# A bidirectional Hyena and pooling encoder layer on one core: the modulated input held as four quarters of 512 tokens, the first quarter rounded and subtracted at the end of the filter stage

## What is computed

```python
mod = silu(c) @ w_ada + b_ada
shift, scale, gate = split(mod, 3)
u = h * (1.0 + scale) + shift                 # 2048 tokens x 1024 channels
proj = u @ w_in + b_in                        # 3072 columns
k_freq = rfft(filters(positions) * decay)     # independent of u
y_h = hyena(short_conv(streams), k_freq)      # two long convolutions by FFT
y_p = pool(pool_in)
out = gate * (concat(y_h * silu(hy_gate), y_p * silu(pool_gate)) @ w_out + b_out)
h = layer_norm(alpha * h + out)
```

## Time and profile before

| | us |
|---|---|
| Median of 3 runs | 1243.82 |
| Lowest and highest | 1240.3 and 1246.71 |
| Time of the profiled execution | 1241.09 |
| Span of its trace | 1239.3 |
| TensorE matmul (PE) busy | 1107.0 (89%) |
| TensorE weight load (PEld) busy | 852.1 (69%) |
| VectorE (DVE) busy | 850.9 (69%) |
| ScalarE (ACT) busy | 569.1 (46%) |
| GpSimd (POOL) busy | 12.5 (1%) |
| Mean granted TensorE clock, share of full | 0.951 |

### The profile page before, as it was taken

How to read it: one execution, slowest core, us unless ns; L and a number is a source line. 1 busy time by engine, 2 the same in 40 slices (tenths; PEclk the granted TensorE clock), 3 DMA queues, 4 the chain that set the end, 5 groups by cost and what they waited for, 6 DMA issues and landing times. The chain is left out here.

```text
span 1239.3 us, 14298 instructions
## 1 busy us (share of the span) xinstructions
PE 1107.0 (89%) x4928; PEld 852.1 (69%) x4928; DVE 850.9 (69%) x1093; ACT 569.1 (46%) x745; POOL 12.5 (1%) x32
## 2 busy tenths in 40 slices
PE   3899589999999999889999988898898748999996
PEld 0277368888888777667888765676676527888884
DVE  6599784555454638359999445646989666787877
ACT  4078643444545345337777434334786633222210
POOL 0001000000000000000000000000000000000000
PEclk8799889999999999999999988999989968999998
DMA  9869953677675445778998578758898597375521
GB/s 350 284 199 310 326 206 120 211 238 245 222 247 170 146 142 188 245 197 254 276 279 244 176 205 259 237 192 240 267 295 249 190 347 226 132 220 163 171 88 64
DMA packets 154990, 273.25 MB, mean 220 GB/s; under 512 B 11488, under 2 KB 49504, under 8 KB 153253
## 3 DMA queue, kind: packets, MB, share of 16 engines
q1 hardware_dynamic: 151461, 266.74, 67.0%
q0 software_dynamic: 3168, 5.51, 1.9%
q10 hardware_dynamic: 288, 0.08, 0.0%
HBM read 178.95 MB, written 98.57 MB: 224 GB/s over the span
## 5 line engine op out<-in xcount | busy, mean ns | idle before, releaser
L176 PE MATMUL u_pp<-u_uhi,prj_whi 128*128 128x512 f32 x768 | 312.6, 407 | 21.5 <-DMA p_first<-in_t_kfirst 10.6
L177 PE MATMUL u_pp<-u_ulo,prj_whi 128*128 128x512 f32 x768 | 307.7, 401 | 0.0
L178 PE MATMUL u_pp<-u_uhi,prj_wlo 128*128 128x512 f32 x768 | 306.9, 400 | 0.0
L176 PEld LDWEIGHTS u_pp<-u_uhi,prj_whi 128*128 128x128 f32 x768 | 148.2, 193 | 64.5 <-issue 20.4
L178 PEld LDWEIGHTS u_pp<-u_uhi,prj_wlo 128*128 128x128 f32 x768 | 147.7, 192 | 35.1
L177 PEld LDWEIGHTS u_pp<-u_ulo,prj_whi 128*128 128x128 f32 x768 | 148.2, 193 | 33.2
L1241 DVE TENSOR_TENSOR p_alo<-p_a,p_ahi 128x1024 fp32r<-128x1024 f32 x32 | 39.2, 1225 | 101.0 <-ACT p_ahi L1182 101.0
L176 PE MATMUL end_ps<-end_whl,prj_whi 128*128 128x512 f32 x256 | 101.2, 395 | 2.4 <-DVE prj_wlo L2136 2.4
L178 PE MATMUL end_ps<-end_whl,prj_wlo 128*128 128x512 f32 x256 | 101.1, 395 | 0.0
L177 PE MATMUL end_ps<-end_whl,prj_whi 128*128 128x512 f32 x256 | 101.0, 395 | 0.0
L1182 ACT ACTIVATE p_ahi<-p_a 128x1024 fp32r<-128x1024 f32 x32 | 34.0, 1061 | 126.3 <-PE p_ps L178 121.7
(11 more groups left out here) (195 smaller groups left out, 1969.5 us busy)
## 6 DMA issues: line engine op xcount, KB each, us to landing
p_a<-kseq SPq DMA_DIRECT2D x32, 512.0 KB, 4.3
kfreq<-p_out SPq DMA_DIRECT2D x32, 512.0 KB, 5.2
xseq<-p_xo SPq DMA_DIRECT2D x32, 512.0 KB, 7.6
p_k_re<-kfreq SPq DMA_DIRECT2D x64, 256.0 KB, 6.1
p_k_im<-kfreq SPq DMA_DIRECT2D x64, 256.0 KB, 4.3
bseq<-p_out SPq DMA_DIRECT2D x32, 512.0 KB, 4.8
prj_ws<-in_t_win SPq DMA_DIRECT2D x24, 512.0 KB
kseq<-prj_row SPq DMA_DIRECT2D x22, 512.0 KB
```

Source lines behind the costliest of these rows:

```text
L176: nc.tensor.matmul(out, w[0], m[0], start=start, stop=False, skip_group_check=True)
L177: nc.tensor.matmul(out, w[0], m[1], start=False, stop=False, skip_group_check=True)
L178: return nc.tensor.matmul(out, w[1], m[0], start=False, stop=stop, skip_group_check=True)
```

## The change

The modulated input is held as four pairs of tiles, one pair (`uhi[c]`, `ulo[c]`) for each quarter of 512 tokens, in place of one pair for all 2048. The first pair is allocated ahead of the filter stage, the others where the single pair was. ScalarE rounds pieces 0 and 1 in the last two slots of its `step` function, each in front of an `evac`, and pieces 2 and 3 behind its last `evac`. DVE subtracts pieces 0 to 3 in the filter stage too: `low_u` of a piece stands behind the `form_u` of the next, and that of piece 3 last. In the third stage pieces 0 to 3 are left out of both streams. An unused function (`form_u_act`) goes. The waits on TensorE are as they were.

```diff
--- before.py
+++ after.py
@@ -584,6 +584,9 @@
             pj.w_low(dve, 0)
             for m in range(4):
                 pj.form_u(dve, m)
+                if m >= 1:
+                    pj.low_u(dve, m - 1)
+            pj.low_u(dve, 3)
 
         @block.scalar
         def _(act):
@@ -602,8 +605,12 @@
             def step(n):
                 if n == N - 3:
                     pj.w_high(act, 0)
+                if n >= N - 2:
+                    pj.high_u(act, n - (N - 2))
 
             staggered(N, (high, 0), (step, 2), (evac, 3))
+            for m in range(2, 4):
+                pj.high_u(act, m)
 
 
 TILES = (0, 1, 2, 3, 16, 20, 17, 21, 18, 22, 19, 23, 4, 5, 6, 7, 8, 12, 9, 13, 10, 14, 11, 15)
@@ -682,6 +689,7 @@
         self.k_stored = xin.sems("k_stored", 3)
         self.xt_in, self.u_done, self.uhi_done, self.ulo_done = (
             xin.sems(n, 8) for n in ("xt_in", "u_done", "uhi_done", "ulo_done"))
+        self.uhi, self.ulo = [], []
         self.w_in, self.consts, self.pad_set, self.eye_in = s.sem("w_in"), s.sem("consts"), s.sem("pad_set"), s.sem("eye_in")
         self.conv_step, self.row_used = s.sem("conv_step"), s.sem("row_used")
         self.whi_done, self.wlo_done, self.prj_done, self.bank_read = (
@@ -691,9 +699,11 @@
         for b in slots:
             eng.wait_ge(self.k_stored[b], 16 * len(range(b, 2 * GS, 3)))
 
-    def hold_u(self, s):
-        self.uhi = s.sb("uhi", [P, KT, L], F32R)
-        self.ulo = s.sb("ulo", [P, KT, L], F32R)
+    def hold_u(self, s, quarters):
+        self.uhi = self.uhi + [s.sb(f"uhi{c}", [P, KT, CH], F32R) for c in quarters]
+        self.ulo = self.ulo + [s.sb(f"ulo{c}", [P, KT, CH], F32R) for c in quarters]
+
+    def hold_banks(self, s):
         self.pp = [s.ps(f"pp{c}", [P, CH]) for c in range(2)]
 
     def load_x(self, sp, m):
@@ -710,26 +720,17 @@
             ins = self.nc.vector.tensor_scalar(x, x, self.scale1[:, k:k + 1], self.shift[:, k:k + 1], ALU.mult, ALU.add)
         ins.then_inc(self.u_done[m % 8], 1)
 
-    def form_u_act(self, act, m):
-        act.wait_ge(self.xt_in[m % 8], 16 * (m // 8) + 16)
-        for e in range(2):
-            k = 2 * (m % 4) + e
-            x = self.xt[m % 8][:, e, :]
-            ins = self.nc.scalar.activation(x, x, ACT.Identity, scale=self.scale1[:, k:k + 1], bias=self.shift[:, k:k + 1])
-        ins.then_inc(self.u_done[m % 8], 1)
-
     def high_u(self, act, m):
         tc, k2 = m // 4, m % 4
         act.wait_ge(self.u_done[m % 8], m // 8 + 1)
-        self.nc.scalar.activation(self.uhi[:, 2 * k2:2 * k2 + 2, tc * CH:(tc + 1) * CH], self.xt[m % 8][:, :, :],
+        self.nc.scalar.activation(self.uhi[tc][:, 2 * k2:2 * k2 + 2, :], self.xt[m % 8][:, :, :],
                                   ACT.Copy).then_inc(self.uhi_done[m % 8], 1)
 
     def low_u(self, dve, m):
         tc, k2 = m // 4, m % 4
         dve.wait_ge(self.uhi_done[m % 8], m // 8 + 1)
-        cols = slice(tc * CH, (tc + 1) * CH)
-        self.nc.vector.tensor_tensor(self.ulo[:, 2 * k2:2 * k2 + 2, cols], self.xt[m % 8][:, :, :],
-                                     f32(self.uhi[:, 2 * k2:2 * k2 + 2, cols]), ALU.subtract).then_inc(self.ulo_done[m % 8], 1)
+        self.nc.vector.tensor_tensor(self.ulo[tc][:, 2 * k2:2 * k2 + 2, :], self.xt[m % 8][:, :, :],
+                                     f32(self.uhi[tc][:, 2 * k2:2 * k2 + 2, :]), ALU.subtract).then_inc(self.ulo_done[m % 8], 1)
 
     def load_consts(self, sp):
         t = self.t
@@ -764,10 +765,9 @@
             if c == 0:
                 pe.wait_ge(self.wlo_done[b], n // 2 + 1)
             after(pe, self.bank_read[bank], q // 2)
-        cols = slice(c * CH, (c + 1) * CH)
         for k in range(4 * half, 4 * half + 4):
             mm = mm3(self.nc, self.pp[bank][:, :], (self.whi[b][:, k, :], self.wlo[b][:, k, :]),
-                     (self.uhi[:, k, cols], self.ulo[:, k, cols]), k == 0, k == KT - 1)
+                     (self.uhi[c][:, k, :], self.ulo[c][:, k, :]), k == 0, k == KT - 1)
         if half == 1:
             mm.then_inc(self.prj_done[bank], 1)
 
@@ -1068,7 +1068,6 @@
         pj.xt += [*a, *out]
         N = 2 * NU
         form_at = {plan.lo + i: range(4 * i, 4 * i + 4) for i in range(4)}
-        by_act = ()
         S = N + 2
 
         def pool_at(step, lag):
@@ -1193,9 +1192,8 @@
                     high(step)
                 if step in form_at:
                     for m in form_at[step]:
-                        if m in by_act:
-                            pj.form_u_act(act, m)
-                        pj.high_u(act, m)
+                        if m >= 4:
+                            pj.high_u(act, m)
                 if step == 8:
                     pl.split_high(act)
                 if 0 <= step - 1 < N:
@@ -1251,9 +1249,9 @@
             for step in range(plan.lo, S):
                 if step in form_at:
                     for m in form_at[step]:
-                        if m >= 4 and m not in by_act:
+                        if m >= 4:
                             pj.form_u(dve, m)
-                        if m >= 1:
+                        if m >= 5:
                             pj.low_u(dve, m - 1)
                 if step == plan.lo + 4:
                     pj.low_u(dve, 15)
@@ -2255,9 +2253,12 @@
                     fl = Filters(nc, f)
                     front(nc, t, fl, tabs, scale1, shift, rows)
                     pj = Projection(nc, t, u, w, scale1, shift)
+                    held_first = Scope(nc, "u0")
+                    pj.hold_u(held_first, (0,))
                     filter_stage1(nc, t, tabs, fl, kseq, pj)
                 held = Scope(nc, "u")
-                pj.hold_u(held)
+                pj.hold_u(held, (1, 2, 3))
+                pj.hold_banks(held)
                 gt = Gated(nc, u, pj, 16, 0)
                 v = Scope(nc, "pool")
                 pl = Pooled(nc, v, pj, 4, 0)
@@ -2265,7 +2266,7 @@
             with v:
                 signal_stage1(nc, tabs, pj, vx, xseq[0], yp, pl, sig)
             with Scope(nc, "tail", "right") as e:
-                with held:
+                with held_first, held:
                     spectrum_product(nc, "p3", tabs, t, pj, xseq[0], kfreq[0], bseq[0], gt, g2, sp1, vx=vx)
                     between_orders(nc, tabs, pj, vx, bseq[0], xseq[1], gt, g2, btw)
                     tail = Tail(nc, t, e, pj, bseq[1], rows)
```

## The result

| | before | after |
|---|---|---|
| Median of 20 runs, us | 1242.76 | 1247.49 |
| Lowest and highest, us | 1238.4, 1247.38 | 1240.98, 1251.88 |
| Span of the profiled execution, us | 1239.3 | 1241.4 |

The ratio of the times is 1.0041, with a 95% interval of 1.0027 to 1.0055: the changed kernel is slower by 4.7 us on the medians, 0.41%, clear of the noise (the interval is 3.4 to 6.8 us). The forecast was 1248.0, from a difference of 4.3 us and a median of before of 1243.82; over twenty runs that median is 1242.76. So the difference is 0.4 us larger than forecast, and the time itself 0.5 us less.

A forecast was written before the change was run, and what follows sets the result against it. DVE's stream, which sets chunk 3's start, was taken to bound the kernel. An opening 4.9 us later less 0.6 us returned made 4.3 us on the median 1243.82: 1248.1, taken as 1248.0, range 1243.0 to 1251.5 us.

The forecast's parts named there:

- The bound: Third stage: DVE's stream sets chunk 3's start, 25.12 us after piece 6 is formed, and everything behind moves with it.
- Steps 1 to 3: Filter stage's end: evac 29 at 141.4, PE's last product at 142.55, DVE's last subtraction ending at 148.6 instead of 143.13.
- rival B: Filter stage's tail: PE's last product at half clock, opening 6.4 us later, 1250.2 if landings return nothing; chance 0.16.
- Step 4: Barrier behind the filter stage: DVE last at 148.6, next stage opens 1.65 us after, at 150.25, 4.9 us later.
- The return in the third stage: Third stage's head: of 4.56 us of DVE work removed, 0.6 us comes back, since DVE waits for loads.
- the 25.12 us of before: Third stage: time from forming piece 6 to chunk 3's start, taken as the same in both kernels.
- The page's figure: Third stage's loads: skill page's estimate of 3.2 us to landing against 4.2 traced; would make the loss 2.7 us.
- A: Rival at the third stage's opening: moved pair rides for nothing, 1.7 us faster, 1242.1; chance 0.05.
- C: Rival beyond 180 us: a later stage absorbs the 4.3 us, leaving 1243.8; chance 0.09.
- D: Third stage: loads land quicker, return 1.5 us, 1247.2; inside the forecast's own spread, forecast with it 0.70.
- a sign of being wrong: Whole trace: prediction wrong if, among other signs, the shift at 200 us differs from that at the end by over 2 us.

The follow-up runs named there:

- dose12: Kernel before with 12 more chained DVE products at the filter stage's end that change no result; +14.7 us, ratio 1.0114.
- before_tabs: Kernel before with the two small tables loaded in the filter stage instead of the third; +0.3 us, ratio 1.0003.
- before_low15: Kernel before with low_u of piece 15 moved ahead of the second weight tile's low part and first convolution; -5.6 us, ratio 0.9958.
- before_byact: Kernel before with form_u of pieces 5, 7, 9, 11, 13 and 15 on ACT instead of DVE; -0.5 us, ratio 1.0011.
- round_last: Changed kernel with ACT's four roundings behind its last evacuation; +7.5 us against the kernel before, ratio 1.0057.
- high_only: Changed kernel with the four roundings behind ACT's last evacuation and the four subtractions back in the third stage; +2.5 us against before, ratio 1.0025.
- early4: Changed kernel with buffers allocated early so pieces 4 to 7 load in the filter stage; +1.4 us against the kernel before, ratio 1.0008.
- tiles_only: Changed kernel with the quarter tiles kept, but rounding and subtraction of pieces 0 to 3 back in the third stage; +0.1 us, ratio 0.9993.
- before_again: Kernel before, unchanged, traced once more; one run, no ratio given.
- experiment 5: Kernel before, unchanged, in a second trace; fourth stage took 101.0 us against 103.6 in the first trace.

## Why the prediction was right

**The bound.** Chunk 3's start sets the time, and DVE's stream sets chunk 3: shown by dose12 (14.03 us at the opening, 14.03 at chunk 3, 14.7 in the time), by before_tabs (an earlier table, no gain) and by before_low15 (one DVE instruction moved, 5.6 us). One half of it was too narrow: DVE depends on ACT at every piece, so that relief of DVE at ACT's cost gives nothing (before_byact). For the forecast that hardly mattered, since the change gives neither engine new work behind the opening. That PE is full from 180 us on holds for the stretches shown; from 900 to 1100 us it is busy for only 164 of 200 us. What dose12 adds is that these later waits moved with the rest.

**Steps 1 to 3, the tail of the filter stage.** All of that part of the kernel stood 0.27 us earlier in the changed trace. With that taken off, evac 29 was forecast at 141.1 and ran at 141.12, the last product at 142.3 and ran at 142.27, `low_u(3)` at 147.1 and ran at 147.12. The half clock of rival B did not come; the matmuls of the last product have their full speed.

**Step 4, the barrier.** I took 1.65 us from DVE's end to the opening; it was 149.59 - 148.34 = 1.25. So the opening moved by 4.5 us, not 4.9. round_last (DVE last) and high_only (ACT last) have 1.25 and 1.24 too. Both of the rows behind the 1.65 were of another kind: the 1.61 of the earlier trace rows counts from the end of a DMA issue, and at the boundary at 54 us of the earlier trace rows SP issued a store behind DVE's end, so that the 1.68 counted from DVE is 1.39 counted from the last to finish:

```profile
53.91 0.25 SPq L357 DMA_DIRECT2D rows<-flt_gate  x1
```

**The return in the third stage.** Forecast 0.6 us, from piece 6 formed 8.05 after the opening instead of 8.63. Measured 15.73 - 7.10 = 8.63 and 19.52 - 11.60 = 7.92: 0.7 us. early4 and high_only show the mechanism from both sides: without the wait for the loads piece 6 comes at +3.3, and with the four subtractions back it comes only 0.25 us later.

**One term left out.** From piece 6 to chunk 3 I took the 25.12 us of before. It was 25.63: ACT's rounding of the second weight tile waited 0.80 us for its load, and DVE 0.41 us for ACT behind it. In tiles_only, where nothing is moved, 0.35 us of the same kind appear (25.47), so most of this term need not come from the moved work. So the sum at chunk 3 was 4.5 - 0.7 + 0.5 = 4.3, the number forecast, with two small errors that cancel; that they do is luck.

**The page's figure.** Piece 4 landed 4.0 us after its issue, 4.2 in the kernel before. From the fit of the Trainium skill ("DMA: Bandwidth & Descriptors", section "Anatomy of one DMA"), which is for transfers issued from GpSimd, an estimate of 3.2 follows for this size. The measurement decides, and the 2.7 us forecast by the page's figure would have been too low.

**The rivals.** A (nothing lost) failed where the prediction said: the loads cannot start before the barrier. B failed at the clock. C is refuted by dose12, and what looked like it in the spans is explained by before_again: the shift is 4.1 us at 200 us and 2.1 at the end, 2.0 apart, just at the limit that the prediction set as a sign of being wrong, and the clock of that one trace makes up for it. D, the quicker landings, came as 0.1 to 0.2 us and not as the 0.9 it needed.

## What to carry to other kernels

Work at the head of a stage that runs while the stage's own loads are under way is nearly free there (0.25 us for four subtractions). Moved ahead of the barrier it delays the opening, here by 4.5 us, and what it leaves behind is a wait for the loads, of which only 0.7 us came back. Before moving work, find the last wait ahead of the point from which the bound engine never stops, and look at what stands in front of it in its stream that it does not need: here one subtraction behind 3.2 us of foreign work was worth 5.6 us, more than any load, table or engine change tried. And when two engines hand pieces to each other, count both before moving work from one to the other.

## What the runs showed of the hardware that was not expected

TensorE's clock after a short pause differs from one execution of the same kernel to the next: before chunk 2 it paused 2.46 us in the first trace of before, ran four matmuls of 0.39 to 0.47 us and then fell to half (PEclk 0.79 in the window shown above), while in the second trace of before it paused 2.49 us and the matmuls after the first kept 0.39 to 0.40 us each. The same happened after 2.18 and 2.16 us in the fourth stage (experiment 5). The Trainium skill ("TensorE: Matmul & The Clock Gate", section "Part 1: The HAM clock gate") says of the start of a kernel that the number of slow matmuls varies from run to run; these traces show such a variation behind a pause in its midst. At chunks 2 and 3 of the first trace each fall costs about 8 matmuls of 0.43 instead of 0.23 us apart, about 1.6 us.

The median over sessions of the kernel before lay between 1242.1 and 1243.9 us, with single runs from 1236.8 to 1252.2, so differences under 2 us were read from the traces' milestones rather than from the times.
